# PEER block kernel: fewer elements in the candidate extraction, another interleave beside it, and gate stores issued from ScalarE's queue

## What is computed

```python
q = (hf @ w_q).reshape(T, PEER_HEADS, 2, PEER_DHALF)            # 8 heads, 2 sides of 64
scores = jnp.einsum('thpd,pnd->thpn', q, sub_keys)              # 128 keys on each side
sv, si = lax.top_k(scores, PEER_TOPK)                           # 16 best of each side
cand = (sv[:, :, 0, :, None] + sv[:, :, 1, None, :]).reshape(T, PEER_HEADS, 256)
cv, ci = lax.top_k(cand, PEER_TOPK)                             # 16 best sums
ia = ci // PEER_TOPK
ib = ci % PEER_TOPK
e_idx = (jnp.take_along_axis(si[:, :, 0], ia, axis=-1) * N_KEYS
         + jnp.take_along_axis(si[:, :, 1], ib, axis=-1))       # expert numbers
gates = jax.nn.softmax(cv, axis=-1)
...
a = jnp.einsum('thkd,td->thk', jnp.take(u_tab, ei, axis=0), xi)
wgt = jax.nn.gelu(a) * gi
out = jnp.einsum('thk,thkd->td', wgt, jnp.take(v_tab, ei, axis=0))
```

## Time and profile before

| | us |
|---|---|
| median of 3 runs | 1747.64 (1747.59 to 1748.58) |
| profiled execution | 1745.57 |
| its span, first to last instruction | 1743.8 |
| TensorE busy | 1621.1 (93%) |
| VectorE busy | 1352.1 (78%) |
| ScalarE busy | 690.2 (40%) |
| GpSimd busy | 652.2 (37%) |

### The profile page before, as it was taken

How to read it: one execution, slowest core, us unless ns; L and a number is a source line. 1 busy time by engine, 2 the same in 40 slices (tenths; PEclk the granted TensorE clock), 3 DMA queues, 4 the chain that set the end, 5 groups by cost and what they waited for, 6 DMA issues and landing times.

```text
span 1743.8 us, 23117 instructions
## 1 busy us (share of the span) xinstructions
PE 1621.1 (93%) x8238; PEld 1370.7 (79%) x8238; DVE 1352.1 (78%) x2718; ACT 690.2 (40%) x1036; POOL 652.2 (37%) x450
## 2 busy tenths in 40 slices
PE   3999999986999999998896999999989999998996
PEld 3787776775899999898895998998966677766774
DVE  7489776987598999989946998988865555646588
ACT  3334565425333344545533343343223333323332
POOL 2010000002216888777552843844814423322301
PEclk9999999997999999999998999999999999999998
DMA  7423225453675656766697988988979999998962
GB/s 272 164 84 111 98 96 181 145 170 141 223 267 175 170 156 148 205 182 165 175 284 258 395 330 320 394 307 317 333 249 371 377 359 354 356 369 293 349 243 103
DMA packets 181682, 422.29 MB, mean 242 GB/s; under 512 B 33600, under 2 KB 66496, under 8 KB 181568
## 3 DMA queue, kind: packets, MB, share of 16 engines
q1 hardware_dynamic: 124368, 281.22, 45.7%
q0 software_dynamic: 57200, 139.58, 24.2%
HBM read 375.55 MB, written 45.15 MB: 241 GB/s over the span
## 4 chain that ended last, share of the span: by engine, by line
PE 69%; DVE 22%; DMA 5%; ACT 2%; issue 2%; SPq 0%; DVEq 0%; ACTq 0%
PE bank L1642 21%; PE bank L1643 20%; PE bank L1644 20%; PE bank L1921 3%; DVE wlo L1274 2%; DVE one L1432 2%; DVE one L1434 2%; DVE one L1436 2%; DMA gates_by_key<-stage 1%; DMA vraw<-in_v_tab_dram 1%; PE bank L1735 1%; DVE raw L964 1%; PE bank L1720 1%; DMA gring<-gates_by_key 1%; DVE eq L1373 1%
## 5 line engine op out<-in xcount | busy, mean ns | idle before, releaser
L1642 PE MATMUL bank<-act_hi,whi 128*128 128x384 f32 (+1 forms) x1352 | 482.6, 357 | 27.1 <-ACT gelz L848 15.6
L1644 PE MATMUL bank<-act_hi,wlo 128*128 128x384 f32 (+1 forms) x1352 | 473.1, 350 | 0.0
L1643 PE MATMUL bank<-act_lo,whi 128*128 128x384 f32 (+1 forms) x1352 | 473.1, 350 | 0.0
L1642 PE MATMUL bank<-vhi,eh 128*128 128x512 f32 x768 | 306.3, 399 | 14.6 <-DVE vlo L1474 14.5
L1643 PE MATMUL bank<-vlo,eh 128*128 128x512 f32 x768 | 302.2, 393 | 0.0
L1644 PE MATMUL bank<-vhi,el 128*128 128x512 f32 x768 | 301.3, 392 | 0.0
L1642 PEld LDWEIGHTS bank<-act_hi,whi 128*128 128x128 f32 x1352 | 256.1, 189 | 46.4 <-issue 22.7
L1474 DVE TENSOR_TENSOR vlo<-vraw,vhi 128x512 fp32r<-128x512 f32 x256 | 175.0, 691 | 130.7 <-ACT vhi L896 129.9
L638 POOL DMA_INDIRECT gates_by_key<-selW,selS x128 | 238.5, 1864 | 77.3 <-issue 52.6
L1643 PEld LDWEIGHTS bank<-act_lo,whi 128*128 128x128 f32 x1352 | 256.2, 190 | 14.0
L1644 PEld LDWEIGHTS bank<-act_hi,wlo 128*128 128x128 f32 x1352 | 255.6, 189 | 13.3
(11 more groups left out here) (236 smaller groups left out, 2022.6 us busy)
## 6 DMA issues: line engine op xcount, KB each, us to landing
raw<-in_u_t_dram SPq DMA_DIRECT2D x128, 512.0 KB, 6.1
vraw<-in_v_tab_dram SPq DMA_DIRECT2D x256, 256.0 KB, 5.8
raw<-in_wblk_dram SPq DMA_DIRECT2D x61, 512.0 KB, 4.1
raw<-in_w_modt_dram SPq DMA_DIRECT2D x48, 512.0 KB, 3.8
gring<-gates_by_key SPq DMA_DIRECT2D x32, 768.0 KB, 9.2
gates_by_key<-stage SPq DMA_DIRECT2D x8, 2048.0 KB, 11.6
gelu_ahead<-gelz SPq DMA_DIRECT2D x20, 768.0 KB, 4.3
gback<-gelu_ahead SPq DMA_DIRECT2D x40, 384.0 KB, 8.2
```

Source lines behind the costliest of these rows:

```text
L1642: mm(o, wh, mh, start=start, stop=False)
L1643: mm(o, wh, ml, start=False, stop=False)
L1644: return mm(o, wl, mh, start=False, stop=stop)
```

## The change

Candidates: the list becomes exactly the 50 pairs with (a+1)(b+1) <= 16, in four parts, so that the chosen numbers of ranks 4g to 4g+3 always lie in the first `WITHIN[g]` = 8, 20, 36, 50 of the list. The values and the numbers of a pair are now added by one operation over both (18 operations of 16 groups instead of 2 x 5 of 8). Extraction: instead of 8 heads x (16 x 54 = 864 elements), six pieces of 256, 640, 576, 576, 800 and 800 elements, three operations each. Interleave: 15 points instead of 17. The last point, with one `low_u` in selects 0 and 1 (now two), and in selects 2 and 3 with two one-hot blocks and two `low_u`, stands behind the select's last operations. Stores: the gate stores move from SyncE's queue to ScalarE's, right behind the stage copy that completes a half.

```diff
-RECTS = [(0, 1, 16), (1, 1, 8), (2, 2, 5), (4, 4, 3), (8, 8, 1)]
-NCAND = sum(na * nb for _, na, nb in RECTS)
+RECTS = [[(0, 1, 0, 4), (1, 1, 0, 2), (2, 2, 0, 1)],
+         [(0, 1, 4, 4), (1, 1, 2, 2), (2, 2, 1, 1), (4, 4, 0, 1)],
+         [(0, 1, 8, 4), (1, 1, 4, 2), (2, 2, 2, 2), (4, 2, 1, 1), (8, 4, 0, 1)],
+         [(0, 1, 12, 4), (1, 1, 6, 2), (2, 1, 4, 1), (4, 1, 2, 1), (6, 2, 1, 1), (12, 4, 0, 1)]]
+PIECES = [(0, 0, 8), (1, 0, 8), (2, 0, 4), (2, 4, 4), (3, 0, 4), (3, 4, 4)]
...
-LOWS = ((1, 1, 1, 1, 1, 1, 1, 1, 1, 1, 1, 1, 1, 1, 1, 1, 0), (1, 2, 1, 3, 1, 2, 1, 1, 1, 2, 1, 2, 1, 2, 1, 2, 0))
-ONES = (0, 2, 0, 2, 0, 2, 1, 1, 1, 1, 1, 1, 1, 1, 1, 1, 0)
+LOWS = ((1, 1, 1, 1, 1, 1, 1, 1, 1, 1, 1, 1, 1, 1, 2), (1, 2, 1, 3, 1, 2, 1, 2, 1, 2, 1, 2, 1, 2, 2))
+ONES = (0, 2, 0, 2, 0, 2, 1, 1, 1, 1, 1, 1, 1, 1, 2)
...
-                if c in STORE_AT:
-                    store_gates(*STORE_AT[c])
...
+                if t0 == TB - TOK:
+                    act.wait_ge(gt_sb, n + 1)
+                    act.dma_start(gates_dram[:, :, P // TB + blk, :],
+                                  stage[:, s].rearrange("p (q f) t -> p q (f t)", f=4)).then_inc(stage_out[s], 16)
...
-                for src, dst in ((sv, cand), (sif, ecand)):
...
+                for a, na, b, nb in [rect for part in RECTS for rect in part]:
+                    shape = [P, 2 * PH, na, nb]
...
+                def piece(i):
+                    g, h0, nh = PIECES[i]
+                    shape = [P, nh, RANKS, WITHIN[g]]
...
-                for h in heads:
-                    beside(8 + h)
-                    if h + 1 < PH:
-                        numbered(h + 1)
-                    dve.wait_ge(eqm_r, 8 * s + (h + 1))
-                    link(nc.vector.tensor_reduce(sel[:, 0, h, :], eq[:, h % 2], AX, ALU.add))
-                    if h + 2 < PH:
-                        compare(h + 2)
-                beside(16)
+                for i in range(NP):
+                    beside(8 + i)
+                    if i + 1 < NP:
+                        numbered(i + 1)
+                    summed(i)
+                    if i + 2 < NP:
+                        compare(i + 2)
...
                 last.then_inc(sel_r, 1)
+                beside(14)
```

More of the change, by code:

```diff
@@ L56 @@
 TAPS_AHEAD = 5
-RECTS = [(0, 1, 16), (1, 1, 8), (2, 2, 5), (4, 4, 3), (8, 8, 1)]
-NCAND = sum(na * nb for _, na, nb in RECTS)
+RECTS = [[(0, 1, 0, 4), (1, 1, 0, 2), (2, 2, 0, 1)],
[3 rows of a table added]
+PAIRS = [[(a + i, b + j) for a, na, b, nb in part for i in range(na) for j in range(nb)] for part in RECTS]
+LISTED = [pair for part in PAIRS for pair in part]
+NCAND = len(LISTED)
+RANKS = TOPK // len(RECTS)
+WITHIN = [sum(len(part) for part in PAIRS[:g + 1]) for g in range(len(RECTS))]
+assert sorted(LISTED) == [(a, b) for a in range(TOPK) for b in range(TOPK) if (a + 1) * (b + 1) <= TOPK]
+assert all(LISTED.index((i, j)) < n for n, (a, b) in enumerate(LISTED)
+           for i in range(a + 1) for j in range(b + 1) if (i, j) != (a, b))
+assert all((a + 1) * (b + 1) > RANKS * g for g in range(len(RECTS)) for a, b in PAIRS[g])
+assert all((a, b) in LISTED[:WITHIN[g]] for g in range(len(RECTS)) for a, b in LISTED if (a + 1) * (b + 1) <= RANKS * (g + 1))
+PIECES = [(0, 0, 8), (1, 0, 8), (2, 0, 4), (2, 4, 4), (3, 0, 4), (3, 4, 4)]
+NP = len(PIECES)
 CH = NK
@@ L161, in build @@
         stage = sb("stage", [P, 2, NK, TB], F32, 120)
-        eq = sb("eq", [P, 2, TOPK, NCAND], F32, 192)
+        eq = sb("eq", [P, 2, TOPK * NCAND], F32, 192)
         selT = sb("selT", [P, 3, P], F32, 199)
@@ L222, in build @@
         keys = sb("keys", [P, 2 * NK], F32, 104)
-        sv = sb("sv", [P, PH, 2, TOPK], F32, 105)
-        si = sb("si", [P, PH, 2, TOPK], U32, 106)
-        sif = sb("sif", [P, PH, 2, TOPK], F32, 107)
+        both_of = sb("both_of", [P, 2 * PH, 2, TOPK], F32, 105)
+        sv, sif = both_of[:, 0:PH], both_of[:, PH:2 * PH]
+        si = sb("si", [P, PH, 2, TOPK], U32, 107)
         cv = sb("cv", [P, PH, TOPK], F32, 108)
@@ L232, in build @@
         selI = sb("selI", [P, 2, P], I32, 111)
-        cand = sb("cand", [P, PH, NCAND], F32, 184)
-        cand2 = sb("cand2", [P, PH, NCAND], F32, 186)
-        ecand = sb("ecand", [P, PH, NCAND], F32, 188)
+        cand_all = sb("cand_all", [P, 2 * PH, NCAND], F32, 184)
+        cand, ecand = cand_all[:, 0:PH], cand_all[:, PH:2 * PH]
+        cand2 = sb("cand2", [P, PH, NCAND], F32, 188)
         gates_flat = nc.dram_tensor("gates_by_key", [NTB * P * NK * TB, 1], F32, kind="Internal").ap()
@@ L476, in zero @@
                              zeros[:].unsqueeze(1).broadcast_to([P, per, HALF])).then_inc(zero_out, 16)
[L478 to L486, removed]
             for c in range(PRE):
@@ L1349, in select @@
                     link(nc.vector.tensor_scalar(sif[:, :, 0, :], sif[:, :, 0, :], float(NK), None, ALU.mult))
-                for src, dst in ((sv, cand), (sif, ecand)):
[L1351 to L1358, removed]
+                off = 0
+                for a, na, b, nb in [rect for part in RECTS for rect in part]:
+                    shape = [P, 2 * PH, na, nb]
+                    last = nc.vector.tensor_tensor(
+                        cand_all[:, :, off:off + na * nb].rearrange("p g (a b) -> p g a b", b=nb),
+                        both_of[:, :, 0, a:a + na].unsqueeze(3).broadcast_to(shape),
+                        both_of[:, :, 1, b:b + nb].unsqueeze(2).broadcast_to(shape), ALU.add)
+                    off += na * nb
                 link(last)
@@ L1368, in select, with compare, numbered, summed @@
                                         ALU.subtract).then_inc(gate_sub, 1)
[L1371 to L1374, removed]
+                def piece(i):
+                    g, h0, nh = PIECES[i]
+                    shape = [P, nh, RANKS, WITHIN[g]]
+                    eqs = eq[:, i % 2, 0:nh * RANKS * WITHIN[g]].rearrange("p (h k c) -> p h k c", h=nh, k=RANKS)
+                    return shape, eqs, slice(h0, h0 + nh), slice(g * RANKS, (g + 1) * RANKS)
+                def compare(i):
+                    shape, eqs, hs, ks = piece(i)
+                    nc.vector.tensor_tensor(eqs, posf[:, hs, ks].unsqueeze(3).broadcast_to(shape),
+                                            iota[:, 0:shape[3]].unsqueeze(1).unsqueeze(1).broadcast_to(shape),
                                             ALU.is_equal).then_inc(eq_r, 1)
[L1377 to L1380, removed]
+                def numbered(i):
+                    shape, eqs, hs, ks = piece(i)
+                    dve.wait_ge(eq_r, NP * s + (i + 1))
+                    nc.vector.tensor_tensor(eqs, eqs, ecand[:, hs, 0:shape[3]].unsqueeze(2).broadcast_to(shape),
                                             ALU.mult).then_inc(eqm_r, 1)
+                def summed(i):
+                    shape, eqs, hs, ks = piece(i)
+                    dve.wait_ge(eqm_r, NP * s + (i + 1))
+                    link(nc.vector.tensor_reduce(sel[:, 0, hs, ks], eqs, AX, ALU.add))
                 compare(0)
```

2 lines of the change are left out of this document (1 added, 1 removed).

## The result

The changed kernel takes 1776.51 us (median of 4 runs, 1773.24 to 1777.64), the one before, on the same chip, 1748.11 us (1747.59 to 1748.78): 1.0157 times the time, 95% interval 1.0142 to 1.0172. The profiled execution took 1776.62 us. The forecast was 1765 (1753 to 1773): the sign and the places were right, the size was not, and the time lies outside the range.

A forecast was written before the change was run, and what follows sets the result against it. Bound: TensorE, with block waits in selects 2 and 3 and the last-gate-store chain setting the first weighing, which carries everything behind it. 1745.57 + 17.5 = 1763.1 profiled; the runs' median is 2.07 higher: 1765 us, range 1753 to 1773.

The forecast's parts named there:

- The waits: TensorE's waits for late one-hot blocks 14, 12, 15 and 10 in selects 2 and 3: 12.9 us a select, together +13.0.
- the waits don't shrink with VectorE's speed: Selects 2 and 3: what VectorE saves, 9.5 to 10.5 us a select, it now waits at `low_u`.
- I take four falls at 1.7 = 6.8 us: Clock falls behind the 6.3 and 3.8 us waits, two of each, at 1.7 us each: 6.8 us.
- the gelu of chunk 79: End of select 3: 889.0 plus 13.0 of waits plus 6.8 of clock falls, so at 908.8.
- The scatters: Before the gathers: they follow GpSimd's `low_u` of chunk 63, move with select 2 and end near 901.5.
- The first gather: Behind the last gate group: starts at about 906.3, bound by TensorE and no more by the scatters, +16.1.
- The store: Last gate store beside gathers and two loads on full DMA engines: 26.7 to 28.2 us, landing at about 934.
- the first weighing: Start of the second product, 8.9 to 10.4 us after the store's landing: at 943 to 944, +17.5 us.
- A: Waits come but the clock holds: +13.0 at chunk 79, gathers +9.3, first weighing +10.7, 1758 us; chance 0.2.
- B: VectorE's saving removes the block waits in selects 2 and 3: first weighing near 899, -27 us, 1721; chance 0.07.
- C: Stores hold up ScalarE's copies and gelus, about 6 us for each of 8: +48 and more, 1813; chance 0.06.
- D: No change: waits only half as large as worked out, just what they replace, 1747.6 us; chance 0.04.

The follow-up runs named there:

- experiment 1: Changed kernel with blocks 8 to 15 of selects 2 and 3 again built one `low_u` earlier, extraction, candidates and stores as changed: 1737.8 us, 0.9957 to the kernel before.
- experiment 2: Kernel before with only the new order of blocks 8 to 15, old extraction, candidates and stores: 1787.67 us, 1.0251 to the kernel before.
- experiment 6: Changed kernel with blocks 14 and 15 put back ahead of the `low_u`, blocks 8 to 13 as changed: 1751.23 us, 1.0018 to the kernel before.
- Experiment 7: Changed kernel with unused matmuls filling three block waits of select 3: 1776.9 us with 28, 48 and 14 of them, 1769.94 us with 16, 28 and 9.
- experiment 8: First gather held until all gate stores have landed: changed kernel 1770.05 us, changed kernel with the old block order 1730.17 us, kernel before 1737.02 us.
- experiment 3: Changed kernel with the gate stores back in SyncE's queue: 1775.61 us, 1.0167 to the kernel before.
- experiment 4: Kernel before with the gate stores issued from ScalarE's queue: 1748.84 us, 1.001 to the kernel before.

## Why the prediction was right in its mechanism and wrong in its size

**Right: the order undoes the gain.** Block 14 can't be ready before the copy of a chunk that waits for step 52, whatever VectorE's speed. The waits were forecast at 6.3, 3.8, 2.3 and 0.5 us in each select; the changed kernel has 6.4, 3.9, 2.3 and 0.5 in select 2, and 6.7, 3.8, 2.3 and 0.5 in select 3. Experiments 1, 2 and 6 show that this order is the whole loss and more: 41 us in the old kernel. One sentence went too far, that the waits don't shrink with VectorE's speed: with the old extraction they are 0.4 to 2 us longer each.

**The step that failed: "I take four falls at 1.7 = 6.8 us".** All six long waits were followed by a fall, those of 2.3 us too, and the falls were longer. By the steps: from the gelu of chunk 44 to that of 55 it took 80.3 us (760.3 - 680.0), and the wait-free 60.9 with 13.1 of waits would be 74.0; from 68 to 79 it took 82.9 (916.7 - 833.8), against 60.9 and 13.8. That leaves 6.3 and 8.2 us, 14.5 in place of 6.8 (12.8 by the windows, which show only the six large falls). So the gelu of chunk 79 came at 916.7, not at 908.8. My price came from one fall behind one wait of 2.42 us, with the remark that a wait of 2.54 had none; one fall was taken for the typical one, and only their number was left open. Experiment 7 shows for the three of select 3 that it is the clock and no other slowness: 6.7 us. For the three of select 2 only the windows say so.

**Smaller: a seventh fall, the store and what follows.** The seventh fall, behind the 2.54 us wait at 805.5 to 808.1, cost 1.7 us (granted clock 0.66, then 0.91 in the 8 us behind it); the kernel before had none there, and shorter waits of select 3 made up for it (73.5 us from the gelu of chunk 55 to that of 68, 73.1 before). The scatters were forecast to end near 901.5 and ended at 893.3; as the gathers waited for TensorE until 914.9, this cost nothing. The first gather went out at 914.94 (forecast 906.3), 0.8 us behind the last group's end (0.1 forecast). The store landed at 944.7, 29.8 us behind that gather (forecast 27.7). The window of the changed kernel over the store:

```profile
915.00:945.00 30.00, 26.80 (x155) 26.44 (x153) 8.62 (x10) 7.69 (x11) 10.39 (x10) 1.00 0.92 341
```

The rate is the one forecast (344), but that is 10.2 MB instead of 9.70: ten gathers were issued before the store landed, not nine. From the landing to the first weighing it took 10.6 us (forecast 8.9 to 10.4): that chunk 87's load was out of the way saved nothing. The first weighing is 11.9 us later than the 943.4 of the forecast: 8.6 from the gather's start, of which 7.9 are the later gelu of chunk 79, nearly all of it the clock; 2.1 from the store; 1.2 behind it. Another 1.6 us were lost behind it (span +31.0, weighing +29.4); in all these kernels 816 to 822 us pass from the first weighing to the end, and I didn't pursue this spread.

**The rivals.** A (the clock holds) is refuted: it fell six times of six. B (faster) named the right condition, and experiment 1 meets it: the waits go, and the kernel is faster than before. But its 1721 us were too low: the scatters ended 9.5 us earlier, not 3 at best, and the gathers follow them, so that the store didn't get the engines for itself. It took the hold of experiment 8 to get within 10 us of it. C is refuted by experiments 3 and 4: eight issues of some 0.5 us. D would have needed waits half as long.

**The page on the queues.** By the rule of the Trainium skill, page "DMA: Bandwidth & Descriptors", section "Issuing engines are not separate DMA queues", the move of the stores would bring nothing. Experiments 3 and 4 agree: no gain in either kernel.

**What the range lacked.** Its upper end stood for six or seven falls of 1.7 us. With the length of a fall left as open as their number, up to twice the one that the trace showed, six of them would be 20.4 us instead of 6.8, and the end would have been near 1779.

## What to carry to other kernels

Work that is taken off an engine is only worth something if the engine can use it: look what stands in its queue ahead of the operation that others wait for, and whether that waits for something later in time. Here one more `low_u` ahead of the blocks cost some four times what the shorter extraction saved. A wait of TensorE of 2 us and more is to be priced with a possible fall of the clock behind it, here half as much again in the sum of six. In the kernels looked at, each wait of 3.8 us or more was followed by one; behind those of 2.4 to 2.7 us it came in some kernels and not in others.

When the last store before a stage is on the chain, look at what starts beside it. Holding the row gathers back until it had landed gave 6.5 to 9.4 us between the medians in three kernels, and the fastest one here, with the shorter extraction, the old order of the blocks and the held gathers, takes 1730.17 us, 0.9884 (0.9855 to 0.9913) of the kernel before.

## What the runs showed of the hardware that I had not expected

- The clock fell behind all six late waits of 2.3 to 6.7 us in the changed kernel, and behind the 2.54 us wait at the start of select 3 as well (0.66 in the 4 us behind it), which it had not done in the kernel before. In the kernel of experiment 2 it fell behind the waits of 4.3 and 7.7 us, and stayed at 1.00 behind those of 2.43 and 2.54 us. A fall cost from 1.4 to 2.9 us, and the length of the wait doesn't order them strictly: behind 3.8 us it was 2.7, behind 3.9 us 1.4.
- The last gate store, 2 MB in runs of 512 bytes, took from 12.5 to 29.4 us from issue to landing: 12.5, 15.6 and 18.2 with the gathers held, 23.5 to 29.4 beside them. Issued 5.5 us later in the changed kernel, it landed at the same time (944.3 and 944.7).
- A 128x128 matmul of two plain f32 tiles stands as two in the trace, 0.11 us apart each (56 in 6.25 us): count two for each when filling a wait.
